# A two-layer RWKV and attention decoder block: adaLN modulations by direct fp32 matmuls in column tiles, at other places of the program

## The reference

```python
def adaln(c, w, b):   # c: [2, 1024] in all, w: [1024, 6144]
    m = silu(c) @ w + b
    return six parts of 1024: shift1, scale1, gate1, shift2, scale2, gate2

h = rms_norm(x, n_mix_pre) * (1 + scale1) + shift1
x = x + gate1 * rms_norm(mix(h), n_mix_post)
h = rms_norm(x, n_ffn_pre) * (1 + scale2) + shift2
x = x + gate2 * rms_norm(ffn(h), n_ffn_post)
```

## Time and profile before

| | |
|---|---|
| median of 3 runs | 2120.48 us (2109.75 to 2122.73) |
| the profiled execution | 2112.75 us, span 2111.0 us |
| PE busy | 1840.9 us (87%) |
| DVE busy | 1400.8 us (66%) |
| ACT busy | 1091.5 us (52%) |
| DMA | 442.90 MB, mean 210 GB/s |
| granted TensorE clock, mean | 0.932 of full |

### The profile page before, as it was taken

The page is one execution under the profiler, slowest core; times in us unless marked ns, Lnnn a source line. Parts: engine busy times, 40 slices in busy tenths (PEclk is TensorE's granted clock), DMA queues, the critical chain, the costliest instruction groups (busy, mean ns, idle before and its releaser), DMA issues.

```text
span 2111.0 us, 32971 instructions
## 1 busy us (share of the span) xinstructions
PE 1840.9 (87%) x11460; PEld 1531.6 (73%) x11460; DVE 1400.8 (66%) x1978; ACT 1091.5 (52%) x1466; POOL 134.4 (6%) x208
## 2 busy tenths in 40 slices
PE   6657787888776999698984999999999999999997
PEld 5546666776665888577973787878787887878785
DVE  6824555444634555583215888888888898989897
ACT  6422222221112444482221877777778787878685
POOL 0022222122200000001100000000000000000000
PEclk9878889889787999899996999999999999999999
DMA  9501111101033555354422898888989897979890
GB/s 403 217 35 36 38 37 37 37 2 47 38 144 117 187 192 182 120 240 182 147 107 120 310 355 323 345 318 338 337 318 358 308 364 301 372 291 373 308 371 37
DMA packets 61371, 442.90 MB, mean 210 GB/s; under 512 B 7008, under 2 KB 8160, under 8 KB 10080
## 3 DMA queue, kind: packets, MB, share of 16 engines
q1 hardware_dynamic: 59184, 437.81, 54.2%
q10 hardware_dynamic: 1584, 2.79, 0.3%
q0 software_dynamic: 512, 1.05, 0.1%
HBM read 438.99 MB, written 2.62 MB: 209 GB/s over the span
## 4 chain that ended last, share of the span: by engine, by line
PE 79%; DVE 11%; issue 4%; ACT 3%; POOL 3%; DMA 1%; ACTq 0%; DVEq 0%; POOLq 0%
PE PS L768 30%; PE PS L794 16%; PE PS L492 4%; PE PS L545 4%; PE PS L837 3%; PE PS L524 3%; PE PS L927 2%; PE PS L625 2%; PE PS L947 2%; PE PS L842 1%; PE PS L504 1%; DVE W L1501 1%; PE PS L782 1%; PE PS L479 1%; DVE LO L1378 1%
## 5 line engine op out<-in xcount | busy, mean ns | idle before, releaser
L1378 DVE TENSOR_TENSOR LO<-W,HI 128x1024 fp32r<-128x1024 f32 x758 | 894.3, 1221 | 122.5 <-ACT HI L979 75.1
L979 ACT ACTIVATE HI<-W 128x1024 fp32r<-128x1024 f32 x758 | 785.8, 1062 | 156.1 <-PE PS L768 83.8
L768 PE MATMUL PS<-HI,XHI 128*128 128x512 f32 x968 | 391.2, 404 | 27.0 <-DVE XLO L1633 13.2
L768 PE MATMUL PS<-HI,XLO 128*128 128x512 f32 x968 | 379.2, 392 | 0.0
L768 PE MATMUL PS<-LO,XHI 128*128 128x512 f32 x968 | 292.9, 391 | 1.3 <-DVE LO L1378 0.6
L768 PEld LDWEIGHTS PS<-HI,XHI 128*128 128x128 f32 x968 | 182.3, 188 | 66.3 <-ACT HI L979 17.9
L768 PEld LDWEIGHTS PS<-LO,XHI 128*128 128x128 f32 x968 | 180.8, 188 | 45.8 <-DVE LO L1378 6.3
L768 PEld LDWEIGHTS PS<-HI,XLO 128*128 128x128 f32 x968 | 182.7, 189 | 34.9
L794 PE MATMUL PS<-HI,HHI 128*128 128x512 f32 x484 | 189.4, 391 | 1.5 <-ACT HHI L1161 1.5
L794 PE MATMUL PS<-HI,HLO 128*128 128x512 f32 x484 | 188.5, 389 | 0.0
L794 PE MATMUL PS<-LO,HHI 128*128 128x512 f32 x484 | 145.5, 389 | 0.0
(11 more groups left out here) (280 smaller groups left out, 2269.3 us busy)
## 6 DMA issues: line engine op xcount, KB each, us to landing
W<-w_exp SPq DMA_DIRECT2D x298, 1024.0 KB, 5.5
W<-w_mod SPq DMA_DIRECT2D x48, 1024.0 KB, 8.9
W<-w_ffn SPq DMA_DIRECT2D x33, 1024.0 KB, 4.8
W<-w_rkv SPq DMA_DIRECT2D x8, 1792.0 KB, 7.3
W<-w_qkv SPq DMA_DIRECT2D x8, 1536.0 KB, 6.8
W<-w_o SPq DMA_DIRECT2D x1, 4096.0 KB, 19.3
W<-w_o SPq DMA_DIRECT2D x1, 3072.0 KB, 9.6
W<-w_qkv SPq DMA_DIRECT2D x8, 256.0 KB, 2.8
```

The source lines that it names most:

```text
L768: last = mm(PS[2 * (s % 2) + g], x[:, 2 * n + k, T * g:T * g + T], w[:, 512 * k:512 * k + 512], start=(n == 0 and k == 0 and i == 0 and le ...
L979: fn(HI[:, u % NBUF], raw_unit(phase, u), ACT.Copy).then_inc(hi_ready, 1)
L1378: tt(LO[:, u % NBUF], raw_unit(phase, u), HI[:, u % NBUF].bitcast(F32), ALU.subtract)\
```

## The change

Modulations no longer pass through HI and LO. `COND` is now 32 columns wide (MW), the two conditions and zeros. PE multiplies each of the eight chunks of a tile directly in fp32 with the load in `W`; chunk k of a load goes to output partitions 32k to 32k+31, a column tile of its own, and adds to that of the tile's other load. ACT copies the whole bank 128x512 to ROW, and the new `join` adds the four tiles in the turning. `mod_used` counts the loads that PE has used and takes the place of `lo_ready` for SP.

In the first modulation the tiles 0 to 3 (EARLY; shift and scale of the first norm) come first, with gains of their own; tiles 4 to 7 stand between the norm sum and the hidden projections, tiles 8 to 11 between these and the first pair projection, which waits for the second gains (`mod_ready` 2). SP issues nine loads, the LoRA block, the two pair blocks (behind the second and third load used), then the other loads through six slots (5 to 10). The second modulation stands behind `project_out`: tiles 0 to 5, `norm_sum(3)`, tiles 6 to 11, and the FFN waits for its gains (`mod_ready` 3); its loads take the ring places that the FFN's had, and these follow them.

```diff
-START = {"mod0": 0, "ffn": 3, "mod1": 3, "exp": 3}
-UNITS = {"mod0": 0, "ffn": 2 * MOD_LOADS, "mod1": 2 * (MOD_LOADS + FFN_LOADS),
-         "exp": 2 * (2 * MOD_LOADS + FFN_LOADS)}
+START = {"mod1": 3, "ffn": (3 + MOD_LOADS) % RING, "exp": 3}
+UNITS = {"ffn": 0, "exp": 2 * FFN_LOADS}
+EARLY = 4
+MW = 32
+def slot(phase, m):
+    if phase == "mod0":
+        return (0, 1, 2, 5, 6, 7, 8, 9)[m] if m < 8 else 5 + (m - 3) % 6
+    return (START[phase] + m) % RING
...
     k["expert_rank"] = NE - np.arange(NE)[None] + 0 * s
-    k["join"] = s % G == np.arange(G)[None]
+    k["join"] = s % MW == np.arange(G)[None]
     return np.concatenate([np.asarray(k[n], np.float32).reshape(P, w) for n, (_, w) in KCON.items()], 1)
...
         MOD = sb("MOD", 2 * 6 * C * G).rearrange("p (l j g) -> p l j g", l=2, g=G)
-        COND = sb("COND", C * G).rearrange("p (c g) -> p c g", g=G)
+        COND = sb("COND", C * MW).rearrange("p (c m) -> p c m", m=MW)
         GAIN = sb("GAIN", 4 * 2 * C * G).rearrange("p (l k c g) -> p l k c g", l=2, k=4, g=G)
...
+        AFTER_XX = 2 * HALF + C * TT
+        ROW = [[W[:, AFTER_XX + 512 * i:AFTER_XX + 512 * i + 512] for i in range(2)],
+               [flat[2][:, 512 * i:512 * i + 512] for i in range(2)]]
         SEL = flat[1][:, D:D + TT].rearrange("p (g s) -> p g s", g=G)
...
-            for m in range(MOD_LOADS):
-                if m >= RING:
-                    sp.wait_ge(lo_ready, 2 * (m - RING + 1))
+            for m in range(9):
                 load("mod0", m, a["w_mod"][0, m])
-            sp.wait_ge(lo_ready, 2 * MOD_LOADS)
             sp.dma_start(LORA, a["w_lora"]).then_inc(lora_full, 16)
+            sp.wait_ge(mod_used, 2)
             pair_block(0, 0)
+            sp.wait_ge(mod_used, 3)
             pair_block(1, 1)
+            for m in range(9, MOD_LOADS):
+                sp.wait_ge(mod_used, m - 5)
+                load("mod0", m, a["w_mod"][0, m])
             with sp.Fori(0, 3) as i:
                 for p in range(2):
...
             sp.wait_ge(state_ready, C)
             sp.wait_ge(state_out, 16 * C)
             sp.wait_ge(z_ready, C)
-            for m in range(FFN_LOADS):
-                if (START["ffn"] + m) % RING == 0 and m < RING:
+            for m in range(MOD_LOADS):
+                if slot("mod1", m) == 0 and m < RING:
                     sp.wait_ge(wo_psum[0], 4)
                 if m >= RING:
+                    sp.wait_ge(mod_used, MOD_LOADS + m - RING + 1)
+                load("mod1", m, a["w_mod"][1, m])
+            for m in range(FFN_LOADS):
+                if m < RING:
+                    sp.wait_ge(mod_used, 2 * MOD_LOADS + m - RING + 1)
+                else:
                     sp.wait_ge(lo_ready, UNITS["ffn"] + 2 * (m - RING + 1))
                 load("ffn", m, a["w_ffn"][m])
-            for m in range(MOD_LOADS):
-                sp.wait_ge(lo_ready, UNITS["mod1"] + 2 * (m - RING + 1))
-                load("mod1", m, a["w_mod"][1, m])
             sp.wait_ge(lo_ready, UNITS["exp"])
...
-            def modulation(l):
-                phase = f"mod{l}"
-                pe.wait_ge(cond_split, l + 1)
-                def turn(t):
-                    pe.wait_ge(row_sbuf, MOD_TILES * l + t + 1)
-                    for f in range(4):
-                        j = 4 * t + f
-                        last = mm(PS[2][:, 2 * j:2 * j + 2], ROW[t % 2][0:4, P * f:P * f + P], con("join")[0:4],
-                                  start=True, stop=True)
-                    last.then_inc(mod_psum, 1)
-                if l == 0:
-                    pe.wait_ge(con_in, 16)
-                for t in range(MOD_TILES):
+            def turn(l, t):
+                pe.wait_ge(row_sbuf, MOD_TILES * l + t + 1)
+                for f in range(4):
+                    j = 4 * t + f
+                    out = PS[4][:, 2 * j:2 * j + 2] if l else PS[0][:, 2 * j:2 * j + 2] if t < EARLY else \
+                        PS[5][:, 2 * (j - 4 * EARLY):2 * (j - 4 * EARLY) + 2]
+                    last = mm(out, ROW[l][t % 2][:, P * f:P * f + P], con("join"), start=True, stop=True)
+                last.then_inc(mod_psum, 1)
+            def modulation(l, lo, hi, turned=True):
+                for t in range(lo, hi):
                     if MOD_TILES * l + t >= 2:
                         pe.wait_ge(row_sbuf, MOD_TILES * l + t - 1)
-                    for n in range(4):
-                        def part(w, first, end):
-                            for k in range(2):
-                                last = mm(PS[t % 2], XHI[:, 2 * n + k, 0:P], w[:, 512 * k:512 * k + 512],
-                                          start=first and k == 0, stop=end and k == 1)
-                            return last
-                        unit(phase, 4 * t + n, 0, lambda w: part(w, n == 0, False), lambda w: part(w, False, n == 3))
-                    if t:
-                        turn(t - 1)
-                turn(MOD_TILES - 1)
+                    for half in range(2):
+                        m = 2 * t + half
+                        arrived(pe, f"mod{l}", m)
+                        w = W[:, slot(f"mod{l}", m) * LOAD:(slot(f"mod{l}", m) + 1) * LOAD]
+                        for k in range(4):
+                            last = mm(PS[6 + t % 2][MW * k:MW * k + MW, :], COND[:, 4 * half + k], w[:, 512 * k:512 * k + 512],
+                                      start=(half == 0), stop=(half == 1))
+                        last.then_inc(mod_used, 1)
+                    if t > lo:
+                        turn(l, t - 1)
+                if turned:
+                    turn(l, hi - 1)
...
-            modulation(0)
+            pe.wait_ge(cond_ready, 2)
+            pe.wait_ge(con_in, 16)
+            modulation(0, 0, EARLY)
             norm_sum(1)
+            modulation(0, EARLY, 8)
             pe.wait_ge(lora_full, 16)
             w1 = LORA.rearrange("p (n k m) -> p n k m", n=3, k=C)
             for n in range(3):
...
                 for kc in range(C):
                     last = mm(PS[2 + n][:, 0:TT], w1[:, n, kc], B[n][:, kc], start=(kc == 0), stop=(kc == C - 1))
                 last.then_inc(hid_psum, 1)
+            modulation(0, 8, MOD_TILES)
             pe.wait_ge(hid_sbuf, 3)
             pe.wait_ge(mixed_ready, 6)
+            pe.wait_ge(mod_ready, 2)
             prep_rkv(0, 0, 0)
             prep_lora(0, 0)
...
             project_out(0, HT)
+            modulation(1, 0, 6, False)
             norm_sum(3)
+            turn(1, 5)
+            modulation(1, 6, MOD_TILES)
...
             pe.wait_ge(x_split, 1)
+            pe.wait_ge(mod_ready, 3)
             swiglu("ffn", 0, 0, G, lambda: None)
...
             norm_sum(4, YT_BANKS)
-            modulation(1)
             norm_sum(5)
...
             act.wait_ge(col_in, 16)
-            fn(COND, col("cond").rearrange("p (c g) -> p c g", g=G), ACT.Silu).then_inc(cond_ready, 1)
+            act.wait_ge(cond_ready, 1)
...
-                act.wait_ge(cond_hi, 2 * l + 1)
-                if l == 0:
-                    act.wait_ge(cond_ready, 1)
-                fn(XHI[:, :, 0:G], COND, ACT.Copy).then_inc(cond_hi, 1)
-            def modulation(l):
-                def row(t):
-                    act.wait_ge(lo_used, UNITS[f"mod{l}"] + 4 * t + 4)
+            def rows(l, lo, hi):
+                for t in range(lo, hi):
+                    act.wait_ge(mod_used, MOD_LOADS * l + 2 * t + 2)
                     if MOD_TILES * l + t >= 2:
                         act.wait_ge(mod_psum, MOD_TILES * l + t - 1)
-                    fn(ROW[t % 2][0:4], PS[t % 2][0:4], ACT.Copy).then_inc(row_sbuf, 1)
-                for t in range(MOD_TILES):
-                    for n in range(4):
-                        split(f"mod{l}", 4 * t + n)
-                        if n == 2 and t:
-                            row(t - 1)
-                row(MOD_TILES - 1)
+                    fn(ROW[l][t % 2], PS[6 + t % 2], ACT.Copy).then_inc(row_sbuf, 1)
             def square(b, src, dst=B[1]):
...
             act.wait_ge(x_in, 16)
+            for b in range(4):
+                square(b, XT[:, 2 * b:2 * b + 2])
+            rows(0, 0, EARLY)
             act.wait_ge(eps_ready, 1)
-            norm(1, XT)
+            norm_root(1)
+            rows(0, EARLY, 8)
             act.wait_ge(hid_psum, 1)
             fn(HID[:, 0], PS[2][:, 0:TT], ACT.Tanh).then_inc(hid_sbuf, 1)
             act.wait_ge(hid_psum, 2)
             fn(HID[:, 1], PS[3][:, 0:TT], ACT.Copy).then_inc(hid_sbuf, 1)
             act.wait_ge(hid_psum, 3)
             fn(HID[:, 2], PS[4][:, 0:TT], ACT.Sigmoid).then_inc(hid_sbuf, 1)
+            rows(0, 8, MOD_TILES)
             def prep_rkv(c):
...
             wo_out(0)
+            rows(1, 0, 5)
             norm(3, XT)
+            rows(1, 5, MOD_TILES)
             def swiglu(phase, base, j, groups):
...
             norm_root(4)
-            condition(1)
-            modulation(1)
             norm(5, XT)
...
```

(34 more changed lines are left out.)

25 lines of the change are left out of this document (11 added, 14 removed).

## The result

| | before | after |
|---|---|---|
| median of the runs, us | 2116.84 (2109.75 to 2122.73, 4 runs) | 2051.49 (2048.83 to 2055.05, 4 runs) |
| ratio, 95% interval | | 0.9694 (0.9655 to 0.9733) |
| profiled execution, span, us | 2111.0 | 2053.3 |
| granted clock of the profiled execution | 0.932 | 0.926 |

The changed kernel is faster by 65.4 us of the medians. 2046 was predicted, with 2028 to 2072 as the range.

A forecast was written before the change was run, and what follows sets the result against it. VectorE's split was taken to pace both modulations, the first also bound by the DMA. Gains of 27.4 and net 42.6 us (62.6 less 20.0) sum to 70.0, giving 2042.7 or 2050.5 us; 2046 taken, range 2028 to 2072.

The forecast's parts named there:

- The price of a load: Both modulations: four direct matmuls in 32-wide column tiles run together, taking 0.9 us a load.
- Both bounds: Price of a modulation load with column tiles two at a time, 1.71 us, or one after another, 3.42 us.
- First modulation: Stage up to the first pair projection, which starts at 87.7 us instead of 115.16: 27.4 us gained.
- rival (3): Inside forecast (together 0.74): DMA 5 us slower per modulation, 2053 us; or PE's full clock sooner, 2 us a stage, 2037.
- The hole of the DMA: During the hidden projections: six ring slots full at 75.2 us, the DMA stands, last load lands at 84.1.
- Second modulation: Moved to the output projection, ahead of the FFN, which starts at 694.5 us instead of 674.5: 20.0 us lost.
- Behind the FFN: From XT's update to the qkv projections, with the modulation gone: 13.0 us instead of 75.6, 62.6 us gained.
- (1): Both modulations: overlap only two-fold or PE at its lower clock, 1.71 us a load, total 2065 us; chance 0.16.
- (2): Both modulations: four tiles share nothing, 3.42 us a load, PE the bound everywhere, total 2139 us; chance 0.07.
- The level: Whole kernel's time: 2042.7 us from the profiled execution, 2050.5 from the median of runs; 2046 taken.

The follow-up runs named there:

- the second execution: The changed kernel run again with nothing edited: median 2044.93 us, ratio 0.9681.
- old_places: Changed kernel's direct matmuls, but both modulations back where they stood in the kernel before, with loads in the old order: 2085.13 us, ratio 0.9853.

## Why the prediction was right

**The price of a load.** Taken 0.86 to 0.9 us from two 64-wide tiles and the output projection's records; measured 0.86 at full clock. Both bounds were then made real: 1.71 taken and measured (7.06 us for four loads with two tiles); 3.42 taken, 3.43 measured. The runs disagree with the order rule of the Trainium skill (TensorE: Matmul & The Clock Gate, Part 3) as the trace of before did: with strict order in which each tile's second pass holds up the next tile, four tiles would have cost what two tiles cost here. In the runs the first records of all four start within 0.02 us, ahead of any second one. They also share better than by the 2.38 times that it gives for three tiles, from which I had estimated 1.1 us a load: 3.43/0.86 is 4.0 times for four.

**First modulation, 27.4 us predicted, 26.3 measured.** Three terms were off by a little, two of them against each other. The norm's sum ended at 35.1 rather than 34.3. Its root waited another 1.28 us for a table load on ACT, which was hidden before and which I had not priced; nothing waited for it, since the hidden projections were held by tile 7. These started at 65.8 rather than 63.1, since the 16th load was used by 64.0 rather than 61.1, at the lower clock and later landed. But they took 10.6 us where I had kept the 13.5 of before: in both kernels 48 records, at a clock of 1.00 instead of 0.78. That is the effect rival (3) had priced at 2 us; here it was 2.9, and it hid the 2.7 us by which they started late. Ends: 76.4, predicted 76.6. The hole of the DMA came as told, the last load landed at 84.9 for 84.1, and the pair projection began at 88.8 for 87.7.

These two clocks (before and after) are the windows of the hidden projections:

```profile
98.22:111.76 13.54, 13.54 (x48) 11.06 (x48) 12.70 (x32) 2.05 (x3) 0.00 (x0) 0.78 0.01 1
```

```profile
65.76:76.37 10.61, 10.61 (x54) 9.09 (x57) 6.51 (x16) 2.29 (x4) 0.00 (x0) 1.00 0.88 365
```

**Second modulation, 20.0 us lost predicted, 22.0 measured** (23.0 in the second execution). The chain was right: the last load, the row copy, XHI, XLO, the gain, the FFN. From the last load's use to the FFN 5.6 us were worked out and 5.5 measured. What is short is the term before it: counted from the output projection's start the last load was used at 76.9 us instead of 74.8, half of it landing later, half of it 1.93 us of matmuls in place of 0.9, at the lower clock.

**Behind the FFN, 62.6 us predicted, 62.8 measured,** and the passage from XT to qkv 12.9 instead of 13.0. It was the largest term and the surest, since it was read from a like passage in the same trace and not built from parts.

**The rivals.** (1) and (2) did not happen, and their times, 2065 and 2139 us, were right within 6.2 and 1.7 us when they were made to (2071.2 and 2140.7). Half of what (1) named, PE at its lower clock in the DMA's gaps, did happen: 1.93 us for a load, near the 1.71 that (1) had. It cost about 1 us at the end of the second modulation and part of the 2.7 us at the 16th load, because in most loads the DMA's 2.5 us cover it.

**The level.** The three terms give 67.1 us where 70.0 were predicted. That I set 2046 between the profiled execution's 2042.7 and the median's 2050.5 was a choice, and how near the number came owes something to luck: the median of one series is 2051.5 (2048.8 to 2055.1), that of the other, on the same program, 2044.9 (2044.3 to 2051.7). The spread of the time mix's clock, 12.7 us between two executions of one program, is larger than all errors of the terms together, and no step of the prediction had it.

## What to carry to other kernels

When a transfer paces a stage, taking work from the engines beside it gives nothing by itself (30.7 us came where an engine was the pace, none where it was the DMA); it makes room, and the gain is in what is moved into that room. Then ask of each moved block what it holds: which slots it stops from coming free, and whether what stands behind it waits for its data or only for a bank or a place in the queue. Halving the moved modulation gave another 21 us, since the FFN behind it used none of it and the passage ahead of the FFN had room for one half. Price a passage by a like passage in the same trace where there is one, and the end of a stage at PE's lower clock where PE has been waiting for loads.

## What the runs showed of the hardware

**A leaner PE loses its clock.** With four tiles sharing a pass PE needs about 1 us of matmuls at full clock for each load of 2.5 us. In old_places, where it waited 1.4 us or less for each load, it was granted 0.66 from 40 to 68 us and 0.58 from 68 to 77, which is the lower level (1.2 GHz) most of the time; in the changed kernel 0.74 from 27.7 to 60 us, with the gap of 10.8 us in it. What stands behind the last load then costs up to double until the clock is back: 1.93 us for 1.06, 3.58 for 1.95, 6.05 for 3.70. Doubling the matmuls held it at 1.00 (2.4 GHz) and gave 4 us back at the end of that stage. The Trainium skill (TensorE: Matmul & The Clock Gate, "HAM oscillation — how this bites in real kernels") tells of the same pattern, compute that is shorter than the wait for its data, so that each next piece starts cold, with waits of about 3 to 5 us. The traces agree in the pattern, but here the clock fell with far shorter waits, 1.16 us ahead of the first load that took 1.94 us in old_places (at 28.60 us), and not every piece was cold (1.06 us at 37.22 and at 57.11).

**Column tiles of direct fp32 matmuls share fully.** Four 32-wide tiles on the same 128 rows: 0.86 us for four matmuls of 512 columns, the time of one; with two tiles the four take 1.71 us and with one 3.43.

**The clock of a long stage in which PE is not always busy is not the same from run to run.** The time mix, with PE busy about 77% of it: 494.8 us at 0.86, 498.9 at 0.84, 507.5 at 0.82, all with the same 4544 matmuls. A difference of 10 us between two profiles of kernels with such a stage proves nothing until the stage is compared by itself.
